# One core, two blocks of layers: the delta stage and the differential attention of the last two layers become one stage of 49 slots, and GpSimd applies the level masks ahead

## What is computed

```
def block(args):                       # diff_attention, queries in 4 blocks of 128
    s = jnp.einsum("bqmd,bkmd->bmqk", q_blk, kf)            # 12 maps, depth 32
    p = jax.nn.softmax(s - slopes[:, None, None] * dist, axis=-1)
    a = p[:, :, 0] - lam * p[:, :, 1]                       # the two maps of a head
    return jnp.einsum("bhqk,bkhe->bqhe", a, vf)

# chunk_gated_delta, once forward and once on the reversed sequence
A = jnp.where(strict, jnp.einsum("bhncd,bhnsd->bhncs", kb, kc) * decay, 0.0)
sol = lax.linalg.triangular_solve(A, rhs, left_side=True, lower=True, unit_diagonal=True)
...
def step(state, inp):                  # from chunk to chunk
    v_new = u_i - w_i @ state
    o = qg_i @ state + aqk_i @ v_new
    state = state * gl_i + kdec_i^T @ v_new
```

## Time and profile before

| | |
|---|---|
| median of 3 runs | 4210.27 us (4207.33 to 4212.7) |
| the profiled execution, whole span | 4209.9 us |
| PE busy | 3901.8 us, 93% |
| DVE busy | 2270.4 us, 54% |
| ACT busy | 1414.5 us, 34% |
| POOL busy | 237.8 us, 6% |
| delta stage of the first of the two layers | 2431.9 to 2645.3 us |
| differential attention of that layer | 2645.3 to 2743.7 us |
| norm of the heads of that layer | 2743.7 to 2763.7 us |
| the other layer: delta, differential attention | 3411.0 to 3623.3, to 3723.7 us |

### The profile page before, as it was taken

The page is one execution under the profiler, slowest core; times in us unless marked ns, Lnnn a source line. Parts: engine busy times, 40 slices in busy tenths (PEclk is TensorE's granted clock), DMA queues, the critical chain, the costliest instruction groups (busy, mean ns, idle before and its releaser), DMA issues. The chain is left out here.

```text
span 4209.9 us, 49789 instructions
## 1 busy us (share of the span) xinstructions
PE 3901.8 (93%) x20649; PEld 3126.2 (74%) x20649; DVE 2270.4 (54%) x3424; ACT 1414.5 (34%) x2074; POOL 237.8 (6%) x212
## 2 busy tenths in 40 slices
PE   7998799999999999899999989889998989898998
PEld 4884667888888777578877778557786768666876
DVE  5625755554564333362267666753475856664375
ACT  2115633111443121252254222432364322343264
POOL 0000210000000000000000032000000023000000
PEclk9998889999999999999999999789999989799998
DMA  5500013343112111123232100022232200012231
GB/s 203 171 31 10 6 41 100 128 134 117 57 56 83 58 58 58 40 81 100 82 100 84 53 4 1 6 71 90 90 100 68 69 7 1 6 61 70 90 100 60
DMA packets 254721, 288.90 MB, mean 69 GB/s; under 512 B 6757, under 2 KB 226940, under 8 KB 254518
## 3 DMA queue, kind: packets, MB, share of 16 engines
q1 hardware_dynamic: 252437, 281.84, 20.8%
q10 hardware_dynamic: 2080, 4.19, 0.3%
HBM read 283.92 MB, written 2.10 MB: 68 GB/s over the span
## 5 line engine op out<-in xcount | busy, mean ns | idle before, releaser
L458 PE MATMUL banks<-h_halves,w_halves 128*128 128x512 f32 x3824 | 1437.4, 376 | 83.1 <-DVE h_halves L257 42.2
L459 PE MATMUL banks<-h_halves,w_halves 128*128 128x512 f32 x3824 | 1429.7, 374 | 0.0
L460 PE MATMUL banks<-h_halves,w_halves 128*128 128x512 f32 x3824 | 1422.9, 372 | 0.0
L458 PEld LDWEIGHTS banks<-h_halves,w_halves 128*128 128x128 f32 x3824 | 735.1, 192 | 234.7 <-issue 84.9
L460 PEld LDWEIGHTS banks<-h_halves,w_halves 128*128 128x128 f32 x3824 | 732.4, 192 | 127.8
L459 PEld LDWEIGHTS banks<-h_halves,w_halves 128*128 128x128 f32 x3824 | 734.6, 192 | 121.1 <-issue 0.5
L257 DVE TENSOR_TENSOR w_halves<-work,w_halves 128x2048 fp32r<-128x2048 f32 (+1 forms) x215 | 488.2, 2271 | 468.7 <-ACT w_halves L252 468.4
L252 ACT ACTIVATE w_halves<-work 128x2048 fp32r<-128x2048 f32 (+1 forms) x215 | 407.2, 1894 | 535.7 <-PE banks L460 401.9
L252 ACT ACTIVATE h_halves<-kept 128x512 fp32r<-128x512 f32 (+1 forms) x520 | 332.5, 666 | 313.4 <-PE banks L460 234.8
L257 DVE TENSOR_TENSOR h_halves<-kept,h_halves 128x512 fp32r<-128x512 f32 (+1 forms) x520 | 361.2, 736 | 138.6 <-ACT h_halves L252 137.9
L950 DVE SCALAR_TENSOR_TENSOR kept<-kept 128x512 f32<-128x512 f32 x280 | 188.2, 744 | 7.7 <-DMA kept<-in_mod_w 7.7
(11 more groups left out here) (367 smaller groups left out, 4548.4 us busy)
## 6 DMA issues: line engine op xcount, KB each, us to landing
work<-in_w_ff SPq DMA_DIRECT2D x64, 1024.0 KB, 5.4
work<-in_ffn_w_in SPq DMA_DIRECT2D x44, 1024.0 KB, 5.1
kept<-in_mod_w SPq DMA_DIRECT2D x40, 1024.0 KB, 5.2
work<-in_odd_w_in SPq DMA_DIRECT2D x24, 1024.0 KB, 5.1
work<-in_w_in SPq DMA_DIRECT2D x24, 1024.0 KB, 5.2
work<-in_ffn_w_out SPq DMA_DIRECT2D x16, 1024.0 KB, 5.2
work<-in_even_w_in SPq DMA_DIRECT2D x13, 1024.0 KB, 5.3
work<-in_odd_w_out SPq DMA_DIRECT2D x8, 1024.0 KB, 5.2
```

Source lines behind the costliest of these rows:

```text
L458: nc.tensor.matmul(o, low[:, k - a, fc], rh[:, tc], start=(k == 0), stop=False)
L459: nc.tensor.matmul(o, high[:, k - a, fc], rl[:, tc], start=False, stop=False)
L460: mm = nc.tensor.matmul(o, high[:, k - a, fc], rh[:, tc], start=False, stop=(k == K - 1))
```

## The change

`diff_stage` is gone, and `delta_stage` becomes `mixer_stage`, which does both. Its loop has 7 x 7 = 49 slots, one for each level, and the seventh round for the end of the last head. The 24 steps of the attention are laid over them, one step every two slots, in a pipeline with fixed lags: `scores` in a slot `t`, `top` and `exps` in `t+1`, `invert`, `rescale` and `subtract` in `t+2`, the two halves of the turn in `t+3`, the copy of its second half, `weigh` and `out` in `t+4`. So an even slot holds `scores`, `invert`, `rescale`, `subtract`, `weigh`, `out` of three different steps, and an odd one `top`, `exps` and the turn.

PSUM has 8 banks for both, so the double banks go. The levels have one bank (`level_bank`) and one bank for the transposes (`x_bank`); the second half of `turn` waits until ACT has copied the first. One pair of score banks, so `scores` of a step waits for `exps` of the step before; one bank for turn and weigh.

The masks of the levels are applied to the matrix before the product, by POOL (`masked_level`, two levels ahead, in three buffers), so DVE's `masked` falls away; ACT copies the result out of PSUM instead (`pairs_copy`, 128x512). `update` is one instruction of 128x512 instead of two. On level 0 the product with the identity is a transpose. In the attention, the factor of the second map goes from DVE (128x512) to ACT (`rescale`), and `out` goes from DVE to ACT; the copy of the turn is cut in two. The products of ones are gone. The transfer of the distances is now at the start of this stage, and POOL waits for it before all else.

```
+    def step_at(t, lag):
+        s, odd = divmod(t + 2 - lag, 2)
+        return s if odd == 0 and 0 <= s < N else None
...
-            def pairs(h, lv, e):
-                ...
-                    old = blocks(h, lv, c * P, P) if lv else core.ident()
+            def pairs(h, lv):
+                m = level_of(h, lv)
+                pe.wait_ge(level_masked, m + 1)
+                if m:
+                    pe.wait_ge(u_done, m)
+                for c in range(4):
+                    o, s = level_bank[:, cc(c)], pl.level[m % 3][:, cc(c)]
+                    if lv:
+                        mm = nc.tensor.matmul(packed(o, lv), s, chunk_blocks(h, lv, c), start=True, stop=True)
+                    else:
+                        mm = nc.tensor.transpose(o, s, core.ident())
                 mm.then_inc(pt_done, 1)
             def turn(h, lv, e):
+                pe.wait_ge(u_done, level_of(h, lv))
+                if turn_of(h, lv, e):
+                    pe.wait_ge(x_done, turn_of(h, lv, e))
-            def products(h, lv, e):
-                pe.wait_ge(pt_masked, step_of(h, lv, e) + 1)
-                pe.wait_ge(x_done, turn_of(h, lv, e) + 1)
+            def products(h, lv):
+                pe.wait_ge(pt_copied, h * (LV - 1) + lv)
+                pe.wait_ge(x_done, turn_of(h, lv, 1) + 1)
...
+            prepare(0, 0)
+            pe.wait_ge(v_copied, 1)
+            pe.wait_ge(dist_made, 1)
+            scores(0)
+            for step in range(1, 4):
+                prepare(0, step)
             for h in range(H + 1):
                 for lv in range(LV):
+                    if h < H and lv:
+                        turn(h, lv, 0)
+                    if h < H:
+                        pairs(h, lv)
+                    if h < H and lv:
+                        turn(h, lv, 1)
                     before(h, lv)
+                    attend(t, 0)          # first half of the turn, or weigh
                     if h < H and lv:
+                        products(h, lv)
                     behind(h, lv)
+                    attend(t, 1)          # scores, or second half of the turn
...
+            for t in range(slots):        # ACT
+                h, lv = divmod(t, LV)
+                if step_at(t, 4) is not None:
+                    copy(step_at(t, 4), 1)
+                if h < H and lv:
+                    kept(h, lv, 0)
+                    pairs_copy(h, lv)
+                    kept(h, lv, 1)
+                if step_at(t, 2) is not None:
+                    rescale(step_at(t, 2))
+                if step_at(t, 3) is not None:
+                    copy(step_at(t, 3), 0)
+                if step_at(t, 4) is not None:
+                    out(step_at(t, 4))
+                if step_at(t, 1) is not None:
+                    exps(step_at(t, 1))   # and the split of two tiles at steps 1 and 9
+                outputs(h - 2)            # on level 0
+                prepare(h + 1, lv - 1)    # on levels 1, 2, 3
...
+            def masked_level(h, lv):      # POOL
+                m = level_of(h, lv)
+                if lv == 0:
+                    pool.wait_ge(s_ready, h + 1)
+                if m >= 3:
+                    pool.wait_ge(pt_done, m - 2)
+                nc.gpsimd.tensor_tensor(c4(pl.level[m % 3]), c4(pl.s[h % 2]), mat(pl.pairs[:, cc(lv)]),
+                                        ALU.mult).then_inc(level_masked, 1)
+            pool.wait_ge(loads_in, 80)
+            nc.gpsimd.tensor_copy(pl.dist16, pl.dist).then_inc(dist_made, 1)
...
+            for t in range(slots):        # DVE
+                top(step_at(t, 1)); invert(step_at(t, 2))
                 # values / states / corrected, low and exponents, queries: as before
-                    masked(h, lv)
                 update(h, lv)
+                subtract(step_at(t, 2))
                 # differences, corrected / states, key_gram, query_gram: as before
```

More of the change, by code:

```diff
@@ L33 @@
 NEG = -1.0e30
-SET = 49
+SET = 50
 GW = 256
@@ L2773, in __init__ @@
         self.u, self.s = [take(1024) for _ in range(3)], [take(512), take(512)]
+        self.level = [take(512) for _ in range(3)]
         self.x, self.pt, self.bm = take(512), take(512), [take(512), take(512)]
@@ new lines, in turn_step, with weigh @@
+            def turn_step(s, part):
+                if part == 0:
+                    pe.wait_ge(subtracted, s + 1)
+                    if s:
+                        pe.wait_ge(out_done, s)
+                else:
+                    pe.wait_ge(turned_copied, 2 * s + 1)
+                for j in range(2):
+                    mm = nc.tensor.transpose(turn_bank[:, cc(j)], pl.both[s % 2][:, cc(2 * part + j)], core.ident())
+                mm.then_inc(turned, 1)
+            def weigh(s):
+                h, i = steps[s]
+                pe.wait_ge(turned_copied, 2 * s + 2)
+                for j in range(4):
+                    mm = nc.tensor.matmul(weigh_bank(half(h)), pl.vt_diff[:, j * DIFF_W + h * HD:j * DIFF_W + (h + 1) * HD],
+                                          pl.at[s % 2][:, cc(j)], start=(j == 0), stop=(j == 3))
+                mm.then_inc(weighted, 1)
@@ new lines, in attend @@
+            def attend(t, place):
+                if place == 0:
+                    for s, work in ((step_at(t, 3), lambda s: turn_step(s, 0)), (step_at(t, 4), weigh)):
+                        if s is not None:
+                            work(s)
+                else:
+                    for s, work in ((step_at(t, 0), scores), (step_at(t, 3), lambda s: turn_step(s, 1))):
+                        if s is not None:
+                            work(s)
+            for b in range(3):
+                for q in range(4):
+                    mm = nc.tensor.transpose(core.ps[:, 5 + b, cc(q)], u2(core, 10 + b)[:, cc(q)], core.ident())
@@ new lines, in rescale, with copy @@
+            def rescale(s):
+                act.wait_ge(inverted, s + 1)
+                second = pl.pr[s % 2][:, SEQ:]
+                nc.scalar.activation(second, second, ACT.Copy, scale=sc(s, 7, 1)).then_inc(rescaled, 1)
+            def copy(s, part):
+                act.wait_ge(turned, 2 * s + part + 1)
+                if part == 0 and s >= 2:
+                    act.wait_ge(weighted, s - 1)
+                nc.scalar.activation(pl.at[s % 2][:, two(part)], turn_bank, ACT.Copy).then_inc(turned_copied, 1)
@@ L3104, in _, with out @@
+            def out(s):
+                h, i = steps[s]
+                act.wait_ge(weighted, s + 1)
+                nc.scalar.activation(u2(core, 4 + h // 2)[half(h), cc(i)], weigh_bank(half(h)), ACT.Copy).then_inc(out_done, 1)
+            split(0)
             for step in range(3):
                 prepare(0, step)
[L3106 to L3113 removed]
+            act.wait_ge(lam_s, 1)
@@ L3179, in _, with split @@
         @block.vector
         def _(dve):
+            chain = Chain(dve, chain_s)
+            def split(t):
+                for n in range(2):
+                    dve.wait_ge(pair_high, 2 * t + n + 1)
+                    nc.vector.scalar_tensor_tensor(out=pl.low[n][t % 2], in0=tiles_of(n, t), scalar=(scale, 1.0)[n],
+                                                   in1=pl.high[n][t % 2].bitcast(F32), op0=ALU.mult,
+                                                   op1=ALU.subtract).then_inc(pair_low, 1)
```

510 lines of the change are left out of this document (213 added, 297 removed).

## The result

The changed kernel takes 4178.1 us (median of four runs, 4173.9 to 4180.1) against 4210.3 (4207.3 to 4212.7): ratio 0.992, 95% interval 0.9906 to 0.9934. The forecast was 4176. The profiled execution has a span of 4176.8 us against 4209.9.

The account below looks back on a forecast made before the run. PE was taken to bound the kernel. Per layer, start 28, head 0 39, five heads 205, end 21.5 and norm 1 gave 294.5 against 311.8 us; twice 17.3 less gave 4176 us, range 4140 to 4209.

Parts of the forecast that it names:

- Rival 1: Merged stage: PE bound with 1 to 3 us of waits in a head, 4150 to 4200 us; chance 0.50.
- Start: Stage's start to the first `turn`: 28 us, before 14.0 + 16.0; PE waits for POOL's slope, then the second preparation follows.
- Head 0: First head of the loop: 39 us, before 27.1; 34 of PE work and waits, 5 more for half clock.
- Five heads: Level loop's five full heads: 41 us each, before 30.7, with 1 to 3 of waits; 205 against 153.3.
- End: Behind the last head: 21.5 us, before 18.9; last attention steps' chain of 17.3 at half clock, beside the recurrence.
- Norm of the heads: Norm behind the mixer, 20.0 us before: 1 us more, as it follows a thin stage instead of a warm one.
- The masks: Level loop: DVE loses 14 instructions, 5.9 us a head; worth nothing by itself, but makes room for the attention.
- the case that GpSimd's cover falls away: Level loop: POOL makes masks two levels ahead; without that cover, 1.28 us a level would lie bare.
- Rival 3: Merged stage: DVE and POOL block each other, 3.6 us a head, so no change, 4200 to 4218 us; chance 0.14.
- The test I named: DVE in the merged stage: `queries` and subtract keep their medians as before, else DVE and POOL block each other.
- Rival 4: Chain through ACT becomes the bound; delay per slot loses the gain at 0.42 us, 4241 us at 0.8; chance 0.16.
- The chances: Whole kernel against before, by over 0.2% (8.4 us): faster 0.78, the same 0.08, slower 0.14.

Follow-up runs that it names:

- Experiment 3: The changed kernel without the two products of slope and distance in each attention step (computation left out): 4150.9 us, ratio 0.9859.
- experiment 1: The changed kernel with the level masks back on VectorE behind the product, none on GpSimd and no ScalarE copy of the product: 4176.9 us, ratio 0.9926.
- experiment 4: The changed kernel with two more small ScalarE copies, 0.53 us together, at the head of each of 36 slots a layer: 4177.7 us, ratio 0.993.
- experiment 9: The changed kernel with every level mask done twice on GpSimd, 42 more operations of 1.27 us a layer: 4184.6 us, ratio 0.9947.
- experiment 7: The changed kernel with the last step's second half of the turns put ahead of the twelve products of results_of_states: 4176.2 us, ratio 0.9923.
- experiment 2: The kernel before, stages unmerged, with masks ahead on GpSimd, ScalarE copying the product in halves, level 0 as a transpose: 4214.6 us, ratio 1.0016.
- experiment 5: The changed kernel with six more small ScalarE copies, 1.6 us together, at the head of each of 36 slots a layer: 4198.8 us, ratio 0.9974.
- experiment 10: The changed kernel with start and end reordered, products of ones in the start, and level masks back on VectorE: 4160.0 us, ratio 0.9877.

## Why the prediction was right, point by point

*The total and the mechanism.* Rival 1, PE bound with 1 to 3 us of waits a head, is what happened: 1.7 us. Experiment 3 shows the bound. Experiments 1, 4 and 9 show that VectorE, ScalarE and GpSimd are not it: more work on each cost nothing, nothing and 6 to 9 us. The others' loads were forecast well: 23.5, 20.8 and 17.3 us a head on DVE, ACT and POOL against 23, 22 and 21. The total of 4176 was off by 2 us, but single terms were off by more and cancelled: against 28, 39, 205 and 21.5 the stage has 30.5, 36.4, 202.8 and 27.0. The sum is 296.7 against 293.5.

*Start, 2.5 us too low.* The order of things was as I had it: the wait for the slope, then the second preparation. The first `turn` stands behind scores(1), and this behind exps(0), as said. What I took too short is the stretch from the masked level to exps(0): I had 1.2 + 1.4 for `top` and `exps` behind 23 us and put the lambdas beside it as hidden. They aren't. DVE does `query_gram`, two products of the lambdas and their sum from 2453.47 to 2456.5, and only then `top(0)`. The first masked level is ready at 21.8 us, earlier than my 23 + 1.2, but exps(0) ends only at 28.0.

*Head 0, 2.6 too high.* I had 34 us of PE with its waits, and 5 more for a clock at half level over 10 us. PE is busy for 33.80 us of 36.4, but that has the slow stretch in it: the mean clock is 0.94, which is about 2 us of loss. So both terms were too high, the work by about 2 and the clock by about 3, and the waits (2.6, not 1) took back a part.

*Five heads, 2.2 too high.* 40.6 us each where I took 41. PE is busy for 38.7 a head, in the middle of my 38.2 to 39.9. The slots: in the third head the `update`s start 6.2, 5.7, 6.5, 6.6, 6.6, 7.4 and 3.3 us after one another, so the lengths were forecast roughly (5.5 to 9 and 3 to 7), though hardly as two kinds. PE is busy for 95.5% of the five heads, as said.

*End, 5.5 too low: the mis-sized term.* I added up the chain of the last attention steps (17.3) and some products, and took the last head's recurrence as there as before, beside it. But both stand in one queue of PE. Before, the last head's end had 68 records and 14.08 us of PE in 18.9; now it is 128 records and 22.70 us in 27.0. The 8.6 us more of PE on top of 18.9 give 27.5. Where a stage is bound by an engine at a low clock, one adds its work, not the longest chain. By experiment 7 the order at the very end is worth little beside that.

*Norm of the heads, 1.4 too low*, 2.4 us a layer: the clock is 0.73 in it, not 0.84.

*Not in my sum at all:* 6.7 us less in stages that weren't touched. My stage was 3.2 us a layer too short and the norm 1.4, together 9.2 in two layers, and those 6.7 us, which may be no more than the difference of two executions, covered most of it: the closeness of 2 us is partly luck.

*The masks, costed at nothing:* right, by experiment 1. In the loop PE never waited for one; at the start it waited 0.4 us for the first (L2794 for L3119). My reason was that they make room for the attention on DVE; experiment 1 shows that not even this is needed. I had named 1.28 us a level for the case that GpSimd's cover falls away; in experiment 2, where it does in places, PE waits 4.8 us for it in a layer's 42 levels.

*Rival 3* happened in part. I wrote that `queries` and subtract would keep their medians, else rival 3. `queries` didn't (694 to 1081 ns). Subtract kept its median (750 and 747), but six of its 48 instructions took 1.16 to 1.37 us, where before none took over 0.76. I had also misread the row of before: "1.1 us lost once" and "the median shows no loss" are wrong, for nine of the 24 `queries` took 1.1 us or more then already. Yet the stage went as rival 1: a `queries` is 0.2 us longer in the mean, on an engine that idles for two fifths of the time. The test I named was of the mechanism and not of its effect on the end. The Trainium skill (SBUF — State Buffer, "Who interferes with whom") has it that a VectorE instruction with two SBUF inputs contends with a GpSimd one that reads SBUF; the trace agrees, for every `queries` of over 1 us ran beside a GpSimd instruction, before and after. My sentence on a VectorE instruction with a single SBUF input left out the page's condition, that it isn't in a mode that uses both pairs of ports; the last section shows such a case. By experiment 9 the contention costs this kernel something only where PE waits for `update`.

*Rival 4* is refuted as it was priced, by experiments 4 and 5: its break-even isn't 0.42 us but lies beyond 1.6, where the kernel still takes 4198.8.

*The chances.* Those of the four rivals give 0.77 for faster and 0.16 for slower, not 0.78 and 0.14, and of rival 3's 4200 to 4218 far less than half counts as faster. Neither changes the forecast.

## What to carry to other kernels

When two stages are merged, the gain lies mostly in the thin ends that the merger fills; the busy loops nearly add up. Here the attention was 98.4 us long as a stage of its own. Inside the other it adds 16.4 us to the start, 9.3 to head 0, 49.5 to the five heads and 8.1 to the end, 83.3 in all. At the 3.13 us of a step before, the 20 steps within the heads would be 62.6, and they cost 58.8. So of the 15 us about 4 came in the loop and 11 at the ends. Cost the new end by adding the work of the engine that bounds it, at the clock that rows show for such ends, and check the new start for what each engine's order puts ahead of the first instruction of the loop: here reordering it was worth 24 us, three quarters of the whole change. A delay on an engine off the path costs only what exceeds its room; measure the room by adding work in two doses before pricing a rival by it.

## What the hardware showed that I had not expected

A `tensor_scalar` with one SBUF input can be held up by GpSimd too. In the start, beside GpSimd's L3096 (2446.36, 1.26 us), L3216 took 1.39 us, where it has 0.43 at 2438.63 and 0.418 in the median:

```profile
2438.63 0.43 DVE L3216 TENSOR_SCALAR work<-work 128x512 f32<-128x512 f32 x1
...
2446.36 1.26 POOL L3096 TENSOR_TENSOR work<-work 128x512 f32<-128x512 f32 x1 [0.65 <-ACT work L2977]
2446.53 1.39 DVE L3216 TENSOR_SCALAR work<-work 128x512 f32<-128x512 f32 x1
```

The six of its 24 instructions that took 1.23 to 1.39 us all began while a product of GpSimd of 1.26 us was under way. I had counted only instructions with two SBUF inputs into rival 3. The Trainium skill (SBUF — State Buffer, "Who interferes with whom") counts `tensor_scalar` among those that may take both port pairs; this row agrees.

`update` of level 0, which writes and reads blocks of one element, takes 1.10 us where that of every other level takes 0.69, with the same number of elements and one input in PSUM:

```profile
2540.87 1.10 DVE L3251 TENSOR_TENSOR work<-work,banks 128x512 f32<-128x512 f32 x1
...
2547.11 0.69 DVE L3251 TENSOR_TENSOR work<-work,banks 128x512 f32<-128x512 f32 x1 [1.33 <-PE banks L2812]
```

PSUM isn't the reason: where the masks are on VectorE, level 0's `update` has both inputs in SBUF and takes 1.07 as well (L3253 of experiment 10). No run here separates the access pattern from other causes of it. And the clock falls in a stage in which PE has no gap: 0.87 of full over 40 us of busy time, in the rows of the input product above.
